# Mixed attention in two blocks with the choice of keys beside the projections, and the convolution's biased tap on ScalarE

## The reference

```
# mixed attention: h is the normed and modulated input
proj = h @ w_in       # c_q 256 | c_kv 128 | k_rope 32 | q_d 512 | k_d 128 | v_d 128 | q_idx 256 | k_idx 32 | w_idx 8
# latent attention, 8 heads: 64 plain and 32 rotated dimensions, values of 64
q  = rms_norm(c_q) @ w_q_b ;  kv = rms_norm(c_kv) @ w_kv_b
y_mla = softmax(q k^T * 96**-0.5, causal) @ v
# sparse attention, 8 heads in 2 groups
idx_score = sum_h relu(q_idx_h . k_idx) * w_idx_h          # causal
sel = top_k(idx_score, 64)                                 # the 64 best keys of each query
y_dsa = softmax(q_d k_d^T * 64**-0.5 - slope_h * |distance|, over sel) @ v_d
x = x + gt1 * rms_norm(concat(y_mla, y_dsa) @ w_o)

# feed-forward with a convolution over 3 tokens, d_ff = 2816
up = h @ w_up ;  up_t = w0 * up_{t-2} + w1 * up_{t-1} + w2 * up_t + conv_b
gate, val = split(up) ;  f = (gelu(gate) * val) @ w_down
```

## Time and profile before

| | |
|---|---|
| median of 3 runs | 3049.86 us (3046.36 to 3059.21) |
| profiled execution | 3045.83 us, span 3044.0 us |
| busy | PE 2676.2 (88%), PEld 2058.7 (68%), DVE 1415.8 (47%), ACT 874.5 (29%), POOL 8.6 us |
| mean granted TensorE clock | 0.941 of full speed |
| read from memory | 721 MB, 237 GB/s over the span |

### The profile page before, as it was taken

The page is one execution under the profiler, slowest core; times in us unless marked ns, Lnnn a source line. Parts: engine busy times, 40 slices in busy tenths (PEclk is TensorE's granted clock), DMA queues, the critical chain, the costliest instruction groups (busy, mean ns, idle before and its releaser), DMA issues. The chain is left out here.

```text
span 3044.0 us, 44362 instructions
## 1 busy us (share of the span) xinstructions
PE 2676.2 (88%) x18088; PEld 2058.7 (68%) x18088; DVE 1415.8 (47%) x1957; ACT 874.5 (29%) x953; POOL 8.6 (0%) x13
## 2 busy tenths in 40 slices
PE   7999899999899965749999999999999799777987
PEld 6999799999789954634444444443444488666987
DVE  5644456475566435443234222121212548245893
ACT  3334344354144211311111212121211452223342
POOL 0000000000000000000000000000000000000000
PEclk9999899999999977759999999999999899888998
DMA  6663636545366320059999999999999624412441
GB/s 214 232 210 111 249 125 238 190 162 213 150 220 210 138 99 23 33 197 371 415 417 415 416 416 416 416 418 417 417 417 417 205 97 126 159 76 83 143 174 69
DMA packets 278879, 724.10 MB, mean 238 GB/s; under 512 B 18913, under 2 KB 177196, under 8 KB 243788
## 3 DMA queue, kind: packets, MB, share of 16 engines
q1 hardware_dynamic: 278434, 722.34, 62.5%
q10 hardware_dynamic: 330, 0.10, 0.0%
HBM read 721.35 MB, written 1.05 MB: 237 GB/s over the span
## 5 line engine op out<-in xcount | busy, mean ns | idle before, releaser
L635 PE MATMUL bank<-h_high,weight_parts 128*128 128x256 f32 x4352 | 789.1, 284 | 23.6 <-DVE weight_parts L623 23.6
L635 PEld LDWEIGHTS bank<-h_high,weight_parts 128*128 128x128 f32 x4352 | 680.3, 191 | 26.9 <-issue 23.0
L623 DVE TENSOR_TENSOR weight_parts<-weight_slots,weight_parts 128x2048 fp32r<-128x2048 f32 x208 | 472.5, 2288 | 245.5 <-ACT weight_parts L617 244.9
L617 ACT ACTIVATE weight_parts<-weight_slots 128x2048 fp32r<-128x2048 f32 x208 | 394.3, 1911 | 393.2 <-DMA weight_slots<-in_ffn_w_in 115.1
L635 PE MATMUL bank<-h_part,weight_parts 128*128 128x256 f32 x1680 | 478.1, 285 | 0.0
L2373 PE MATMUL bank<-weight_slots,item_x 128*64 128x512 f32 x2176 | 475.9, 595 | 0.7 <-ACT item_x L2446 0.7
L2529 DVE TENSOR_TENSOR expert_sum_then_keys<-bank,expert_sum_then_keys 128x512 f32<-128x512 f32 x136 | 84.5, 683 | 625.4 <-PE bank L2412 625.4
L2373 PEld LDWEIGHTS bank<-weight_slots,item_x 128*64 128x64 f32 x2176 | 153.7, 137 | 298.6 <-issue 297.7
L635 PEld LDWEIGHTS bank<-h_part,weight_parts 128*128 128x128 f32 x1680 | 321.4, 191 | 0.1
L635 PE MATMUL bank<-hidden_high,weight_parts 128*128 (+1 forms) x1760 | 305.2, 278 | 5.5 <-DVE weight_parts L623 5.5
L635 PEld LDWEIGHTS bank<-hidden_high,weight_parts 128*128 128x128 f32 x1760 | 268.3, 189 | 5.8 <-issue 5.8
(11 more groups left out here) (489 smaller groups left out, 2711.5 us busy)
## 6 DMA issues: line engine op xcount, KB each, us to landing
weight_slots<-in_w_mlp SPq DMA_DIRECT2D x408, 1024.0 KB, 21.0
weight_slots<-in_ffn_w_in SPq DMA_DIRECT2D x88, 1024.0 KB, 5.1
weight_slots<-in_ffn_w_out SPq DMA_DIRECT2D x44, 1024.0 KB, 7.1
weight_slots<-in_ffn_w_up SPq DMA_DIRECT2D x22, 1024.0 KB, 5.1
weight_slots<-in_a_w_in SPq DMA_DIRECT2D x16, 1024.0 KB, 6.7
weight_slots<-in_w_in SPq DMA_DIRECT2D x16, 1024.0 KB, 5.7
weight_slots<-in_ffn_w_down SPq DMA_DIRECT2D x11, 1024.0 KB, 6.1
weight_slots<-in_a_w_out SPq DMA_DIRECT2D x8, 1024.0 KB, 15.8
```

The source lines that it names most:

```text
L617: K.nc.scalar.activation(high, source, ACT.Copy).then_inc(K.high_written.sem, 1)
L623: K.nc.vector.tensor_tensor(low, place, high.bitcast(F32), ALU.subtract)\
L635: m = K.nc.tensor.matmul(out, stationary[a], moving[b], start=start and n == 0, stop=stop and n == 2, **flags)
```

## The change

Mixed attention gets two large blocks instead of eight small ones.

`mixed_inputs` joins the projections, the norms of the latents, the expansion and the choice of keys. TensorE's order: the index queries first (the angle matmuls between their two halves), index keys and weights, latent queries, index scores of the first query block, key latent, index scores of the second, sparse key, query pairs with the sums of squares between, sparse values, then the expansion with plain and swapped banks by turns, keys, values. The fourfold index key is made by VectorE instead of GpSimd. Index tensors, sparse key and the values are copied by ScalarE instead of VectorE. VectorE does the choice of both query blocks in the meantime, then the norms, and writes the sparse biases (both query blocks) before the attention starts.

`mixed_heads` has the four attentions (pieces 0 to 3: latent and sparse for each query block) in one block, with scores of later pieces ahead of the values of earlier ones. ScalarE copies the outputs instead of VectorE. The temporary tables lie in the unused end of the weight memory and in `mixed`.

In `feed_forward` the body of `middle.dve` is cut in two, `dve` (scaling) and `finish` (the rest). For the convolution `dve` stands between the two splits and `finish` behind them; for SiLU the order stays. `ConvGate` applies the biased tap on ScalarE, by four Identity activations with scale and bias, behind the two high parts; the later taps are done for the gate first and then for the value, and the GELU is signalled after the gate's.

```diff
             with dve.Fori(0, trips) as i:
                 for b, (units, at) in enumerate(loop_up):
-                    for g in range(2):
-                        split(i, 4, 3 + 2 * b + g, units[g], 2 * b + g)
-                    middle.dve(dve, i, dve.snap(i * 2 + b), b, (first_up[1], loop_up[0][1])[b], hid, hid_high, hid_low)
+                    pair, at_pair = dve.snap(i * 2 + b), (first_up[1], loop_up[0][1])[b]
+                    split(i, 4, 3 + 2 * b, units[0], 2 * b)
+                    if middle.between:
+                        middle.dve(dve, i, pair, b, at_pair)
+                    split(i, 4, 4 + 2 * b, units[1], 2 * b + 1)
+                    if not middle.between:
+                        middle.dve(dve, i, pair, b, at_pair)
+                    middle.finish(dve, pair, b, hid, hid_high, hid_low)
...
 class ConvGate:
+    links, between = 5, True
     def act(self, act, i, b, at):
+        act.wait_ge(K.banks.free[up], i + (up_free + 2))
+        for n, tile in enumerate(self.tiles(act, pair)):
+            m = nc.scalar.activation(self.buf[:, b, n, :], self.scaled[:, n, :], ACT.Identity, bias=K.param("ffn_conv_b", tile),
+                                     scale=K.param("conv_w", tile + 2 * 2 * FF // P))
+        m.then_inc(K.last_taps.sem, 1)
         act.wait_ge(K.taps.sem, i * 2 + (K.taps.base + b + 1))
...
-        for out, ps, tile in tiles:
-            m = v.tensor_scalar(out, ps, K.param("conv_w", tile + 2 * 2 * FF // P), K.param("ffn_conv_b", tile),
-                                ALU.mult, ALU.add)
-        K.vsteps.link(m)
+    def finish(self, dve, pair, b, hid, high, low):
+        dve.wait_ge(K.last_taps.sem, pair + (K.last_taps.base + 1))
+        for g in range(2):
+            for n in (2 * g, 2 * g + 1):
+                m = v.scalar_tensor_tensor(out[:, 1:], self.scaled[:, n, 0:S - 1], K.param("conv_w", tiles[n] + 2 * FF // P),
+                                           out[:, 1:], ALU.mult, ALU.add)
+            K.vsteps.link(m)
...
+def mixed_inputs(K, a, W, T):
...
+            project(ps[0][:, 0:S], columns(1184, P))
+            pe.wait_ge(pos_float, 1)
...
+            project(ps[1][:, 0:S], lambda t: W.w_k_four[:, t, :])
...
+            project(ps[2][:, S:2 * S], columns(P, P)).then_inc(banks.full[2], 1)
+            index_scores(0)
...
+            project(ps[3][0:96, S:2 * S], columns(320, 96)).then_inc(banks.full[3], 1)
+            index_scores(1)
...
+            pe.wait_ge(*latents_scaled(1))
+            pe.wait_ge(*arranged_q(1))
+            for j in range(4):
+                for w, at in ((w_q, plain_at[j]), (W.w_q_swapped, swapped_at[j])):
...
+            select(0)
+            banks.ready(dve, c_kv_at)
...
+            select(1)
...
+            V.scalar_tensor_tensor(c_kv, c_kv, K.param("g_kv_a"), rstd_kv, ALU.mult, ALU.mult).then_inc(latents_scaled.sem, 1)
...
+            bias(0)
...
+def mixed_heads(K, T, w_o):
+    score_banks, turned_banks, out_banks = ((0, 1), (2, 3), (4, 5, 6, 7), (4, 5, 6, 7)), ((0, 1), (2, 3), (1, 3, 0, 2), (4, 5, 6, 7)), (0, 2, 1, 3)
...
+        def _(sp):
+            w_o.issue(sp)
...
+            scores(0); scores(1); scores(2)                 # TensorE (one call to a line in the source)
+            turn(0); values(0); turn(1); scores(3); values(1); turn(2); values(2); turn(3); values(3)
...
+            exponential(0); exponential(1); turned(0); turned(1)                # ScalarE
+            exponential(2); output(0); output(1); turned(2); exponential(3); output(2); turned(3); output(3)
...
+            scores(0); scores(1); normalize(0); scores(2)                       # VectorE
+            normalize(1); scores(3); normalize(2); normalize(3)
```

More of the change, by code:

```diff
@@ L1916, in expand_latents @@
[L1916 to L1923 removed]
+            sp.dma_start(self.w_in[:, 4 * i:4 * i + 4, :], view[:, 4 * i:4 * i + 4, :]).then_inc(self.w_in_loaded[i], 16)
@@ L2013, in _ @@
+            output(0)
+            output(1)
+            turned(2)
+            exponential(3)
+            output(2)
+            turned(3)
+            output(3)
         @block.vector
@@ L2039 @@
+            scores(0)
+            scores(1)
+            normalize(0)
+            scores(2)
+            normalize(1)
+            scores(3)
+            normalize(2)
+            normalize(3)
+    for signal in (maxima, exponentials, weights_written):
+        signal.done(12)
 EXPERTS, CHOSEN = 32, 4
```

727 lines of the change are left out of this document (433 added, 294 removed).

## The result

The kernel after takes 2978.89 us in the median of 4 runs (2977.38 to 2983.94), against 3048.11 us (3043.82 to 3059.21) for the kernel before, run on the same chip: a ratio of 0.9774, with a 95% interval of 0.976 to 0.9789. The forecast was 2975 us in a range of 2962 to 2993. The profiled execution has a span of 2977.5 us against 3044.0, so 66.5 us are to be found in the trace.

What follows compares the result with a forecast made beforehand. Mixed attention's stages, each held by another engine, and VectorE in the convolution's up loop were taken as exposed. Savings of 39.6 + 19.4 + 15.5 = 74.5 us from 3049.86 gave 2975 us, range 2962 to 2993.

Steps and rivals of the forecast that it cites:

- Start of part 1: Mixed attention's first projection waits for its weights alone and starts at 1092.2 us, where before it started at 1098.1.
- part 1: Projections, choice and expansion in one block: the choice runs beside TensorE's stream, saving 39.6 us (bounds 36 to 42).
- rival D: VectorE's choice of keys is late by 10 us in part 1, time 2985 us; chance 0.06.
- Part 2: Four attention pieces in a pipeline take 39.5 us instead of 58.9, saving 19.4; bounds 38.2 to 49 us.
- rival B: TensorE goes cold in the attention pipeline, which then saves 10 us, time 2985 us; chance 0.13.
- the bound of 49: Length in us of the four-piece attention pipeline if TensorE is cold throughout, with transposes and values at about double.
- Part 3: Convolution's up loop, biased tap on ScalarE: turns of 11.7 us, ten taking 117 against 133, saving 15.5 us.
- Rival C: In the convolution loop ScalarE's operations exceed the split covering them; saving 4 us, time 2987 us; chance 0.08.
- the part's own lower bound: Convolution loop saves only 9 us if the four Identity operations and their registers take 2.9 us.
- The table loads: Convolution loop: of 0.95 us delay every second turn, nothing or 0.1 is left; no room for a 1.38 us drain.
- Rival F: Gain lost in front of the experts if their first weights wait for something else; about 3048 us; chance 0.015.
- rival E: Denser stream costs TensorE its clock in projections and convolution loop: 75 us at 0.72, 193 at 0.5; chance 0.015.

Runs made afterwards that it cites:

- the positions first: Kernel after, but TensorE waits for the converted positions before its first projection, as the kernel before did: 2978.92 us, ratio 0.978.
- the three edits: Kernel after with piece 3's exponentials earlier, gate and value taps signalled apart, and the convolution's last pair behind the down weights: 2957.73 us, ratio 0.9701.
- the last kernel: Kernel after with the three edits, plus TensorE's idle time in the attention pipeline filled with 14 and 10 constant matmuls: 2961.8 us, ratio 0.9706.
- the kernel with the filling on the old order: Kernel after with TensorE's idle time in the attention pipeline filled with 28 and 10 constant matmuls: 2982.92 us, ratio 0.9792.

## Why the prediction was right, step by step

- **Start of part 1.** Put at 1092.2 from GpSimd's start, measured 1090.58, all of the difference from an input that was ready 1.6 us earlier. Right.
- **TensorE's stream sets part 1, and VectorE keeps up.** Right: no idle time ahead of the expansion; the cover is 4.5 us where 3.5 was worked out (rival D didn't come about). Making the choice twice as long turned the cover into the 9 us wait that it should. Part 1: 39.6 forecast, 38.7 measured. The difference is the projections' clock. Its mean from 1098 to 1150 was 0.97, where 1.00 was expected: one full bank took 8.84 us where others took 7.17.

```profile
1104.13 3.63 PE L1827 MATMUL bank<-weight_slots,h_normed 128*128 128x8 f32 x32
1107.62 8.84 PE L1827 MATMUL bank<-h_normed,weight_slots 128*128 128x256 f32 x32
```

```profile
1108.00:1112.00 4.00, 4.00 (x13) 3.21 (x12) 0.00 (x0) 0.26 (x2) 0.00 (x0) 0.57 0.01 4
```

  The clock fell with TensorE busy without a gap, right behind the narrow matmuls of the index weights (8 columns), which the change moved from the end of the projections into their middle. In ten of the eleven profiles with this order the bank behind them took 8.84 us; with the positions first it took 7.15. No run put those matmuls elsewhere, so that they are the cause is not shown.
- **Part 2.** 19.4 forecast, 18.3 measured (40.64 us for 39.5). The order followed was right in what it named as the hold-up, ScalarE's copies of piece 2 ahead of piece 3's exponentials. Counted from 1171.36, its steps up to 15.0 us came within 0.1 us of the trace. The first that was late is the scores of piece 3, done at 24.0 for 22.4, as the sparse scores took 5.65 us at 0.50. The last is the values, done at 39.4 for 36.9, as they took 3.64 us at 0.50.

  The step that was mis-sized is the clock. I stayed near the warm end, with 1.3 us for the clock, "because the new gaps are at most 2.3 us"; the gap behind the values of piece 0 was 3.26 us, and the clock was at 0.50 for some 20 of the 40.6 us. So rival B came about in part: the Trainium skill's rule (TensorE: Matmul & The Clock Gate, Part 1: The HAM clock gate) was the better guide to the first fall. The second, behind idle times of 1 us at most, neither had. With a clock of 1.00 and the order of the three edits the stage was 1.8 us shorter, 34.25 for 36.07.

  Rival B's price, 10 us, and the bound of 49 were reckoned too high. They rest on 3.67 us for 16 transposes "over both levels", which would be 7 at the lower one. The row of before was at the lower level throughout, in the window of exactly its length:

```profile
1262.70:1266.37 3.67, 3.67 (x16) 3.15 (x16) 2.24 (x6) 2.07 (x5) 0.00 (x0) 0.50 0.00 0
```

  In the pipeline 16 such transposes took 3.67 us at 0.50 too, and 3.06 at 1.00 in the last kernel, where VectorE's normalising paces them: the lower clock costs 0.6 us there and not 3.
- **Part 3.** 15.5 forecast, 15.2 measured alone (its interval is 6 us wide to each side) and 13.9 in the trace of the kernel after. Four Identity operations took 2.08 us, at a pitch of 0.5, above the 1.7 taken from rows of 0.31 (a pitch; one operation took 0.41) and 0.47; exposed are 0.30 us a turn instead of 0.2, so the turn is 11.82 in the mean of nine (2776.57 to 2882.97) for 11.7. The last pair loses 2.15 us in front of the taps, where 0.5 was put: that is the term that was mis-sized. Rival C didn't come about: its second wait on ScalarE is 0.3 us. Its price, 4 us saved, stood on no row; the part's own lower bound was 9.
- **The table loads.** No load was added, and behind the nine between 2762 and 2884 no split in the turns waited at all, for the 0.95 every second turn of before; the one wait at L623, 0.59 us, stands ahead of the first scaling. The drain that the Trainium skill adds to a load (ScalarE: Activation LUTs, What ACT_TABLE_LOAD costs) doesn't show here: ScalarE's idle time ahead of the nine loads is 0.2 us in all.
- **Nothing of the gain is hidden.** Rival F is out: with mixed attention alone changed, 57.0 us arrive at the end for a forecast of 59.0. What wasn't foreseen is that untouched stages differ by up to 6 us between profiles, so the sum of the landmarks, 72.5 with the early input, and the difference of the spans, 66.5, needn't meet. The medians were 69.2 apart.
- **The clock in dense stretches (rival E).** 0.97 in the projections and 1.00 in the loop: out, but for the 1.7 us of that one bank.
- **The sum and the range.** 74.5 us forecast, 69.2 measured: all three parts came out a little short (0.9, 1.1 and 1.6 by the trace), each for a reason above. The low end of the range was added up wrongly: the best bounds, 42, 20.7 and 18, make 80.7 us and not 82, which moves that end by 1 us and decides nothing.

## What to carry to other kernels

When stages held by different engines are laid side by side, add up the stream of the engine that gives the length, and work out for the others by when each result is wanted: the difference is the cover, and here it held to within a microsecond. In an order written by hand look for ready work that stands behind work that isn't, as each such place was worth some microseconds here. Most idle times of TensorE of 3 us or more cost more than themselves here, because the matmuls behind them ran at the lower clock; but the lower clock only costs where TensorE is what the others wait for. Before reading a difference of a few microseconds out of two profiles, look at what an untouched stretch does between them.

## What the runs showed of the hardware

- Idle times of TensorE and the clock behind them, in these kernels: 3.26 us, 5.1 us and 9.1 us were each followed by 0.50, in the first case from 1184 to 1200 though TensorE was busy again after 1185.7, and the last two by some 3 us of lost time each. Filling the 3.26 us with matmuls kept the clock at 1.00. At the first row of the cross-attention's keys, eight idle times of 2.93 to 3.78 us were followed by a row of 15.74 us for 64 matmul records and five of 1.99 to 2.23 by one of 14.05, but so was one of 3.56.
- The clock also fell without such an idle time: at 1207 in the kernel after, and at 1208 in the kernel with the filling on the old order, behind idle times of 0.33 to 1.02 us; and at about 1108 in the kernel after with TensorE busy throughout, right behind 32 matmul records of 8 columns.
- What the lower clock costs: 16 transposes of 128x128 took 3.67 us at 0.50 and 3.06 at 1.00, where they waited for VectorE in between; the 32 matmul records of the last piece's values, which wait for nothing in between, took 3.64 (most of it at 0.50) and 1.97.
- Identity with scale and bias per partition, 128x256 from SBUF, took 0.587 us and came at a pitch of 0.5 us.
- A matmul of 128x128 by 128x128 in float32 took 0.233 us in a row of them at the upper clock, as two records.
